# Gate products of a first block's merge, 20 of 32 made early in plain fp32 between the mixers' products and kept in DRAM

## The reference, cut to what matters

```python
h = x @ w_in                        # a_q .. d: inputs of four mixers; gate: 4 * 1024 columns
y = [mixer_a(...), mixer_b(...),    # each (512, 256): dilated attention, attention over 128 selected keys,
     mixer_c(...), mixer_d(...)]    # gated linear attention in chunks of 64, delta rule in chunks of 128
m = sum(sigmoid(gate[n]) * (y[n] @ w_branch[n]) for n in range(4))
x = layer_norm(ALPHA * x + m @ w_out)
```

## Time and profile before

| | |
|---|---|
| median of 3 runs | 3668.62 us (3665.24 to 3679.7) |
| profiled execution, its own time | 3665.9 us |
| its span | 3664.1 us, 33431 instructions |
| mean granted clock of TensorE | 0.882 |
| busy: TensorE, weight load | 3048.2 us (83%), 2257.0 us (62%) |
| busy: VectorE, ScalarE, GpSimd | 1734.7 us (47%), 646.1 us (18%), 1522.0 us (42%) |

### The profile page before, as it was taken

How to read it: one execution, slowest core, us unless ns; L and a number is a source line. 1 busy time by engine, 2 the same in 40 slices (tenths; PEclk the granted TensorE clock), 3 DMA queues, 4 the chain that set the end, 5 groups by cost and what they waited for, 6 DMA issues and landing times. The chain is left out here.

```text
span 3664.1 us, 33431 instructions
## 1 busy us (share of the span) xinstructions
PE 3048.2 (83%) x12858; PEld 2257.0 (62%) x12858; DVE 1734.7 (47%) x2065; ACT 646.1 (18%) x1005; POOL 1522.0 (42%) x430
## 2 busy tenths in 40 slices
PE   6939448899879999394689989999785689989998
PEld 5715237588556666273258867878562368768877
DVE  2174455444266666413464427860214554438840
ACT  0012210100135554303130010000102220010000
POOL 5600000277311111262017756767451037657776
PEclk9955569799979999696699999999896799989999
DMA  3300000122248887221202222222221212212223
GB/s 136 134 14 31 1 0 1 47 92 92 94 183 324 329 317 270 88 91 51 28 12 92 95 78 80 92 92 92 78 80 39 28 42 97 92 58 92 97 87 115
DMA packets 77126, 353.82 MB, mean 97 GB/s; under 512 B 30908, under 2 KB 31292, under 8 KB 38374
## 3 DMA queue, kind: packets, MB, share of 16 engines
q1 hardware_dynamic: 62824, 333.03, 25.4%
q10 hardware_dynamic: 2902, 10.13, 0.9%
q0 software_dynamic: 11232, 8.43, 0.8%
HBM read 357.39 MB, written 30.83 MB: 106 GB/s over the span
## 5 line engine op out<-in xcount | busy, mean ns | idle before, releaser
L129 POOL TENSOR_TENSOR w_hi<-w_raw,w_zero 128x2048 fp32r<-128x2048 f32 x174 | 627.6, 3607 | 1697.9 <-PE bank L156 1645.3
L156 PE MATMUL bank<-xh,w_hi 128*128 128x512 f32 x1864 | 750.1, 402 | 93.5 <-DVE xl L404 50.1
L132 POOL TENSOR_TENSOR w_lo<-w_raw,w_hi 128x2048 fp32r<-128x2048 f32 x174 | 813.2, 4674 | 13.7
L157 PE MATMUL bank<-xl,w_hi 128*128 128x512 f32 x1864 | 745.8, 400 | 0.0
L158 PE MATMUL bank<-xh,w_lo 128*128 128x512 f32 x1864 | 745.2, 400 | 0.0
L156 PEld LDWEIGHTS bank<-xh,w_hi 128*128 128x128 f32 x1864 | 355.3, 191 | 199.4 <-issue 44.0
L158 PEld LDWEIGHTS bank<-xh,w_lo 128*128 128x128 f32 x1864 | 355.3, 191 | 87.6
L157 PEld LDWEIGHTS bank<-xl,w_hi 128*128 128x128 f32 x1864 | 356.1, 191 | 84.8
L499 DVE TENSOR_TENSOR part<-sig,bank 128x512 f32<-128x512 f32 x96 | 66.1, 688 | 381.7 <-PE bank L158 381.3
L2121 DVE TENSOR_TENSOR fl<-work,fh 128x512 fp32r<-128x512 f32 x44 | 211.2, 4800 | 1.5
L536 DVE SCALAR_TENSOR_TENSOR res<-res,bank 128x512 f32<-128x512 f32 x40 | 27.5, 688 | 377.1 <-PE bank L158 377.1
(11 more groups left out here) (497 smaller groups left out, 4800.4 us busy)
## 6 DMA issues: line engine op xcount, KB each, us to landing
w_raw<-weights SPq DMA_DIRECT2D x216, 1024.0 KB, 4.8
raw<-weights SPq DMA_DIRECT2D x51, 1024.0 KB, 6.3
res<-weights SPq DMA_DIRECT2D x26, 1024.0 KB, 6.1
distance_bias<-distance_bias_once ACTq DMA_DIRECT2D x8, 512.0 KB
na_bias<-grid_bias SPq DMA_DIRECT2D x16, 240.0 KB, 7.0
strips<-distance_bias SPq DMA_DIRECT2D x8, 448.0 KB, 3.2
raw<-picked_rows SPq DMA_DIRECT2D x6, 512.0 KB, 5.9
tabs<-tables SPq DMA_DIRECT2D x2, 1408.0 KB, 6.4
```

The source lines that it names most:

```text
L129: pool.tensor_tensor(self.hi[:, s, :], self.raw[:, s, :], self.zero[:, 0:1].to_broadcast([128, CHUNK]), ALU.add).then_inc(self.rounded, 1)
L132: pool.tensor_tensor(self.lo[:, s, :], self.raw[:, s, :], self.hi[:, s, :].bitcast(F32), ALU.subtract).then_inc(self.split, 1)
L156: self.released(pe.matmul(out, hi, moving[0], start=start, stop=False))
L157: pe.matmul(out, hi, moving[1], start=False, stop=False)
```

## The change

`EARLY` holds 20 of the 32 gates, all u but those with u % 8 in (1, 4, 7). Their 160 blocks are now made by a new class, `EarlyGates`, as plain fp32 products of the unsplit weights in `w_raw` with an unsplit x, which SP loads (2 MB) as the selection begins. They are spread over the mixers' stages. TensorE gets 48 blocks behind the index products; in the attention 2, 1, 1, 2, 1, 1, 0 and 0 at the end of eight iterations in turn (32 in all); 16 behind mixer C's first product; 8 in C's head norm; and 16, 16 and 24 in mixer D's first three stages. ScalarE copies each finished gate out of bank 6 or 7 (bank 7 alone in the attention) at the end of its own part of the stage (in the attention after every eighth iteration), SP stores it to DRAM (256 KB) and after each second one loads the next chunk. A bank's next gate waits for the copy of the one before; in mixer D's third stage the three gates use banks 7, 6 and 7. That stage ends with SP's wait for the stores.

In the first merge ScalarE loads the kept gates from DRAM, four slots ahead, and applies the sigmoid in place; TensorE makes only the branch product of an early gate. `w_hi` and `w_lo` (32 KB of each partition) exist now only around project, the merge and what follows; in the mixers their room holds x and two copied gates. So project splits no chunk for the merge; the merge's first two chunks are loaded during `delta_chunks` and split when the merge begins. A barrier and the clearing of the new semaphores stand behind mixer D. The chunks in DRAM are laid out anew: 13 for project (the last one half padding), 10 early, 14 for the late gates, branches and `w_out`, 37 as before.

The diff, cut:

```diff
+LATE_GATES = (1, 4, 7)
+EARLY = [u for u in range(4 * KT) if u % 8 not in LATE_GATES]
+EARLY_CHUNKS = len(EARLY) // 2
...
+class EarlyGates:
...
+    def load(self, sp, chunk):
+        sp.dma_start(self.k.ws.raw[:, chunk % 2, :], self.k.ws.dram[self.first + chunk, :, :]).then_inc(
+            self.loaded[chunk % 2], 16)
+
+    def begin(self, sp):
+        sp.dma_start(self.x[:, :, :], self.k.dram["xT"]).then_inc(self.x_in, 16)
+        for chunk in range(2):
+            self.load(sp, chunk)
+
+    def fill(self, pe, n):
+        if self.blocks == 0:
+            pe.wait_ge(self.x_in, 16)
+        for b in range(self.blocks, self.blocks + n):
+            j, t = divmod(b, KT)
+            c = b // 16
+            if b % 16 == 0:
+                pe.wait_ge(self.loaded[c % 2], 16 * (c // 2 + 1))
+            if t == 0 and self.banks[j] in self.banks[:j]:
+                before = max(i for i in range(j) if self.banks[i] == self.banks[j])
+                pe.wait_ge(self.copied, before + 1)
+            mm = pe.matmul(self.k.bank[self.banks[j]][:, :], self.k.ws.raw[:, c % 2, 128 * (b % 16):128 * (b % 16) + 128],
+                           self.x[:, t, :], start=t == 0, stop=t == KT - 1)
+            if t == KT - 1:
+                mm.then_inc(self.made, 1)
+        self.blocks += n
+
+    def copy(self, act, n):
+        for j in range(self.n_copied, self.n_copied + n):
+            act.wait_ge(self.made, j + 1)
+            if j >= 2:
+                act.wait_ge(self.stored[j % 2], 16 * (j // 2))
+            act.activation(self.rows[:, j % 2, :], self.k.bank[self.banks[j]][:, :], ACT.Copy).then_inc(self.copied, 1)
+        self.n_copied += n
+
+    def move(self, sp, n):
+        for j in range(self.n_stored, self.n_stored + n):
+            sp.wait_ge(self.copied, j + 1)
+            sp.dma_start(self.out[j, :, :], self.rows[:, j % 2, :]).then_inc(self.stored[j % 2], 16)
+            if j % 2 and j // 2 + 2 < self.tiles // 2:
+                self.load(sp, j // 2 + 2)
+        self.n_stored += n
+
+    def end(self, sp):
+        assert self.n_stored == self.tiles
+        for s in self.stored:
+            sp.wait_ge(s, 8 * self.tiles)
+
+    def clear(self, nc):
+        assert self.n_copied == self.tiles and self.blocks == KT * self.tiles
+        for s in (self.x_in, self.made, self.copied, *self.loaded, *self.stored):
+            nc.sync.sem_clear(s)
+        nc.all_engine_barrier()
 
...
-                            last = ws.product(pe, g[:, :], (k.xh[:, t, :], k.xl[:, t, :]), t == 0, t == KT - 1)
-                        last.then_inc(gate_ready, 1)
+                        if u not in early:
+                            for t in range(KT):
+                                last = ws.product(pe, g[:, :], (k.xh[:, t, :], k.xl[:, t, :]), t == 0, t == KT - 1)
+                            last.then_inc(gate_ready, 1)
                         if u == 0:
...
             def _(act):
+                def ahead_load(e):
+                    act.dma_start(ahead[:, e % 4, :], early_dram[e, :, :]).then_inc(ahead_in[e % 4], 16)
+
+                for e in range(min(4, len(early))):
+                    ahead_load(e)
...
-                    act.wait_ge(gate_ready, u + 1)
+                    if u in early:
+                        e = early_before(u)
+                        act.wait_ge(ahead_in[e % 4], 16 * (e // 4 + 1))
+                        act.activation(ahead[:, e % 4, :], ahead[:, e % 4, :], ACT.Sigmoid).then_inc(sigmoid_ready, 1)
+                        if e >= 1 and e + 3 < len(early):
+                            act.wait_ge(banks_free, early[e - 1] + 1)
+                            ahead_load(e + 3)
+                        continue
+                    act.wait_ge(gate_ready, late_before(u) + 1)
                     if u >= 2:
                         act.wait_ge(banks_free, u - 1)
                     act.activation(sig[:, u % 2, :], k.bank[2 * (u % 2)][:, :], ACT.Sigmoid).then_inc(
...
+                        gate = ahead[:, early_before(u) % 4, :] if u in early else sig[:, u % 2, :]
...
+                if gates and s % 2 and s > 1:
+                    gates.move(sp, 1)
+            if gates:
+                gates.move(sp, 1)
...
+                if gates and i < n_units:
+                    gates.fill(pe, (2, 1, 1, 2, 1, 1, 0, 0)[i % 8])
...
+                if gates and i % 8 == 7:
+                    gates.copy(act, 1)
...
+            k.gates.fill(pe, 48)
...
+            k.gates.begin(sp)
+            k.gates.move(sp, 6)
...
+            k.gates.copy(act, 6)
...
+                k.gates.fill(pe, 24)
...
+            def _(sp):
+                k.gates.move(sp, 3)
+                k.gates.end(sp)
 
...
+        @block.sync
+        def _(sp):
+            k.ws.to_load = k.ws.n_loaded + SLOTS
+            k.ws.load(sp)
...
+        gate_dram = nc.dram_tensor("early_gates", (len(EARLY), 128, SEQ), F32, kind="Internal").ap()
+        gate_sems = ctx.enter_context(ExitStack())
+        k.gates = EarlyGates(k, nc, gate_sems, PROJECT_CHUNKS, len(EARLY),
+                             [7 if 6 <= j < 10 else 6 + j % 2 for j in range(len(EARLY))], gate_dram)
+        k.ws.limit = PROJECT_CHUNKS
         with memory(k, yb=(KT, SEQ)) as k.yb:
...
+                k.ws.blocks, k.ws.skipped = 16 * PROJECT_CHUNKS, EARLY_CHUNKS
+                k.ws.limit = FIRST_CHUNKS - EARLY_CHUNKS
+                with memory(k, whole_x=(KT, SEQ), gate_rows=(2, SEQ)) as (k.gates.x, k.gates.rows):
+                    mixers_ab(k, pj, av, bias_dram)
+                    mixer_c(k, pj, cv)
+                    mixer_d(k, pj, av, cv)
+                    k.gates.clear(nc)
+                    gate_sems.close()
+            with halves_of_weights(k):
+                merge(k, ALPHA, k.dram["xT"], EARLY, gate_dram)
+        ctx.enter_context(halves_of_weights(k))
```

More of the change, by code:

```diff
@@ L167, in product_tm, with halves_of_weights, __init__ @@
         return last
+@contextmanager
+def halves_of_weights(k):
+    with memory(k, w_hi=("r", SLOTS, CHUNK), w_lo=("r", SLOTS, CHUNK)) as (k.ws.hi, k.ws.lo):
+        yield
+class EarlyGates:
+    def __init__(self, k, nc, ctx, first_chunk, tiles, banks, out):
+        self.k, self.first, self.tiles, self.banks, self.out = k, first_chunk, tiles, banks, out
+        self.loaded = [ctx.enter_context(nc.semaphore(f"gate_w_loaded{s}")) for s in range(2)]
+        self.x_in = ctx.enter_context(nc.semaphore("gate_x_in"))
+        self.made = ctx.enter_context(nc.semaphore("gate_made"))
+        self.copied = ctx.enter_context(nc.semaphore("gate_copied"))
+        self.stored = [ctx.enter_context(nc.semaphore(f"gate_stored{s}")) for s in range(2)]
+        self.blocks = self.n_copied = self.n_stored = 0
+    def load(self, sp, chunk):
[44 more added lines that the diff above has]
+        nc.all_engine_barrier()
@@ L437, in _, with merge @@
                 run["vector"](dve, *sems)
-def merge(k, scale_residual, x_dram=None):
+def merge(k, scale_residual, x_dram=None, early=(), early_dram=None):
     ws = k.ws
+    n_late = 4 * KT - len(early)
     with memory(k, yh=("r", KT, SEQ), yl=("r", KT, SEQ), mh=("r", KT, SEQ), ml=("r", KT, SEQ), sig=(2, SEQ),
-                part=(2, SEQ)) as (yh, yl, mh, ml, sig, part):
-        ws.plan(KT * 40)
+                part=(2, SEQ), ahead=(4, SEQ)) as (yh, yl, mh, ml, sig, part, ahead):
+        ws.plan(KT * n_late + 8 * KT)
         with stage(k, "gate_ready", "sigmoid_ready", "branch_ready", "banks_free", "branch_rounded", "merge_order",
-                   "branch_split", "x_in") as (block, gate_ready, sigmoid_ready, branch_ready, banks_free, rounded,
-                                               order, branch_split, x_in):
+                   "branch_split", "x_in", "ahead_in0", "ahead_in1", "ahead_in2", "ahead_in3") as (
+                block, gate_ready, sigmoid_ready, branch_ready, banks_free, rounded, order, branch_split, x_in,
+                *ahead_in):
+            late_before = lambda u: sum(1 for v in range(u) if v not in early)
+            early_before = lambda u: sum(1 for v in range(u) if v in early)
             @block.sync
@@ L896, in _ @@
                           stop=True).then_inc(gate_ready, 1)
+                k.gates.fill(pe, 16)
+            @block.sync
+            def _(sp):
+                k.gates.move(sp, 2)
             @block.scalar
@@ L909, in _ @@
                 act.activation(ku[:, :], tmp[:, :], ACT.Exp).then_inc(decays_ready, 1)
+                k.gates.copy(act, 2)
             @block.vector
@@ L1002, in mixer_c @@
     head_norm(k, [dict(src=k.yb[:, 4 + p, :], scale=1.0 / 64, eps=k.eps[:, 1:2], finish=finish(p))
-                  for p in range(2)])
+                  for p in range(2)], k.gates)
 def mixer_d(k, pj, av, cv):
@@ L1027, in mixer_d, with _ @@
         with stage(k, "vector_order") as (block, order):
+            @block.tensor
+            def _(pe):
+                k.gates.fill(pe, 16)
+            @block.scalar
```

(10 more changed lines are left out.)

48 lines of the change are left out of this document (26 added, 22 removed).

## The result

The changed kernel takes 3554.37 us (median of 4 runs, 3552.13 to 3556.49) against 3668.11 in the runs beside it: a ratio of 0.968, 95% interval 0.966 to 0.971.

A forecast was written before the change was run, and what follows sets the result against it. TensorE was taken to bound the merge and, at a low clock, the attention; VectorE and ScalarE the small stages. -112.0 + 8 + 16.2 + 0 - 18 + 28.7 = -77.1 us gave 3592, range 3562 to 3642.

The forecast's parts named there:

- The price of a rounded block, 0.70: Merge: a block is three rounded products of 0.23 us each, so 160 blocks leaving save 112.0 us.
- the term for everything behind the first block: From `moe`'s start on: 0 us, as the change was said to touch only two parts of the first block.
- Merge, -87.8: First block's merge: -112.0 us for 160 blocks leaving, +8 for waits on VectorE, +16.2 for its start.
- Selection, 0: Selection: 48 early blocks end at 260 us, hidden behind VectorE's search until 266.2, so no change.
- Attention, -18: First block's attention: early blocks lift TensorE's clock to the high level, a head takes 10.75 us instead of 13.53.
- Small stages, +28.7: Mixers C and D: early blocks lengthen five small stages, less 2 us for a warm start, plus 1 for the barrier.
- The token shift: Mixer D: 16 early blocks take 13.9 us plus a copy of 0.6, making the stage 2.7 us longer.
- The last stage: Mixer D's third stage: 16 of 24 blocks hidden, the third tile waits for ScalarE's copy: +13.7 us, 9 to 18.
- Project, left out as "up to 2 us": Project: no longer splits a chunk for the merge, may end up to 2 us earlier; not counted in the sum.
- The attention did not stay low: Rival, attention: the clock stays at 0.50, +55 us instead of -18, 3665 in all; chance 0.11.
- early blocks ran at 0.87 us each where dense and warm: Rival, all early blocks: they run at the low clock everywhere, 1.73 us each, +79 us, 3747 in all; chance 0.05.
- VectorE was not the merge's bound: Rival, merge: VectorE's adds and casts wait out GpSimd's divide, 47 us of waits instead of 8, 3631; chance 0.09.

The follow-up runs named there:

- a_halves_on: The changed kernel with 32-byte pads around the split weights, putting them back on multiples of 64 bytes as before the change: 3594.93 us, ratio 0.980.
- b_halves_off: The kernel before the change with w_zero allocated ahead of w_hi, so the split weights lie 32 bytes off multiples of 64: 3619.72 us, ratio 0.986.
- a_banks8: The changed kernel with four pairs of banks instead of two in all merges: 3547.20 us, ratio 0.966.

## Why the prediction was wrong, step by step

**The price of a rounded block, 0.70, was the step that failed, and with it the term for everything behind the first block, which stood at nothing without a reason.** I took 0.70 from the earlier trace rows for what leaves the merge, and, unsaid, as the same for all that stays. It is 0.68 in the changed kernel. For the 160 blocks that leave, this changes nothing. Behind `moe`'s start some 6400 of these matmuls stand in dense rows; from start to start they take 1495.0 us before and 1451.9 in the changed kernel, 43 us or 6.7 ns each, where that part as a whole gained 38.2. "The change touches only two parts of the first block" was true of instructions and not of addresses. The diff showed that `w_hi` and `w_lo` were allocated elsewhere, and the part by part account never asked what that does to those who read them. Put back, the kernel takes 3594.93 us, 3 us from the forecast of 3592 and inside its range. That closeness is in part luck, as the terms below show.

**The sum within the first block** was -77.1, measured -72.3, and -78.2 in a_halves_on, which is the like comparison. There the attention gave 5.1 us too little (-12.9), and the merge 2.4, project 2.6 and the rest 1.2 more than forecast, so that the misses nearly cancelled. The terms:

*Merge, -87.8.* -84.8; -90.2 in a_halves_on, whose TensorE waits are 7.1 us in 3, against the 8 that I had stepped through. With closer matmuls VectorE is late more often: 13.0 us in 5. The faster clockwork of one engine went into waits for another. The start is as forecast, 725.17 - 708.94 = 16.2 us:

```profile
708.99 3.83 POOL L133 TENSOR_TENSOR w_hi<-w_raw,w_zero 128x2048 fp32r<-128x2048 f32 x1 [545.55 <-POOLq L245]
709.40 3.97 DVE L589 TENSOR_TENSOR yl<-yb,yh 128x512 fp32r<-128x512 f32 x1
...
712.90 4.82 POOL L136 TENSOR_TENSOR w_lo<-w_raw,w_hi 128x2048 fp32r<-128x2048 f32 x1
713.29 4.71 DVE L588 CAST yh<-yb 128x512 fp32r<-128x512 f32 x1
...
718.04 0.69 DVE L589 TENSOR_TENSOR yl<-yb,yh 128x512 fp32r<-128x512 f32 x1
...
725.17 0.79 PE L160 MATMUL bank<-yh,w_hi 128*128 128x512 f32 x1 [26.16 <-DVE yl L589]
```

Eight casts and eight differences cost 16 us because two of them end with GpSimd's two halves of the divide, 3.97 and 4.71 us instead of 0.69 and 0.43. The Trainium skill (SBUF — State Buffer, Terms, shared port pair) says that VectorE and GpSimd share a pair of ports by an exclusive lock and that the loser blocks for the whole instruction; these rows agree, for a cast too.

*Selection, 0.* Right: 84.48 us before and after.

*Attention, -18.* The likeliest case was the right one, the clock at 1.00, but the stage gave 9.6. In order of time, eight iterations (two heads) of TensorE:

```profile
286.10 1.98 PE L214 MATMUL bank<-whole_x,w_raw 128*128 128x512 f32 x4
288.01 0.70 PE L681 MATMUL bank<-pj 64*128 64x256 f32 x2
...
290.02 1.13 PE L214 MATMUL bank<-whole_x,w_raw 128*128 128x512 f32 x2
291.08 0.91 PE L681 MATMUL bank<-pj 64*128 64x384 f32 x2
...
308.82 0.55 PE L689 MATMUL bank<-consts,att_p 128*128 128x128 f32 x3 [0.89 <-DVE att_p L751]
...
309.98 1.98 PE L214 MATMUL bank<-whole_x,w_raw 128*128 128x512 f32 x4
```

From 286.10 to 309.98 are 23.9 us, 11.9 a head, where I had 10.75. The early blocks do not stand in a dense row: two take 1.91 us to the next instruction's start and a single one 1.06, 8.06 us for eight instead of 6.96. TensorE waits 0.89 us for VectorE where I allowed none. The rest is 7.5 a head, against my 7.3. Together 2.4 us per two heads, 9.5 in the stage. And the clock was at 1.00 for four of seven stretches only. The size differs between executions: 101.2 to 110.3 us in eight profiled ones that have the same code for this stage, the shortest at a clock of 0.96 over 262 to 366 us and the longest at 0.87. All are above the forecast's 96.

*Small stages, +28.7.* +31.5, and +28.2 in a_halves_on. The token shift was to start warm; it starts after 2.05 us of idle TensorE at the change of stage, and its 16 blocks take 15.67 us instead of 13.9:

```profile
433.24 15.67 PE L214 MATMUL bank<-whole_x,w_raw 128*128 128x512 f32 x32 [2.05 <-PEq L258]
...
448.95 0.60 ACT L225 ACTIVATE gate_rows<-bank 128x512 f32<-128x512 f32 x1 [6.27 <-PE bank L214]
```

(In a_halves_on, after an idle stretch just as long, they took 13.97 us: the clock was 1.00 from 432 to 436 us there, and 0.66 from 433 to 437 here.) The chunks' stage after the first of mixer C gained nothing from a warm start (forecast -2, here +1.9, and 0.0 in a_halves_on). The last stage came as told, step by step: 12.34 us of idle behind ScalarE, eight blocks, at first cold, in 9.10 us (I had 6 + 3.9 = 9.9), copy, store.

```profile
479.13 13.90 PE L214 MATMUL bank<-whole_x,w_raw 128*128 128x512 f32 x32
...
504.72 1.08 ACT L225 ACTIVATE gate_rows<-bank 128x512 f32<-128x512 f32 x2 [3.66 <-DVE pj L1284]
...
505.37 9.10 PE L214 MATMUL bank<-whole_x,w_raw 128*128 128x512 f32 x16 [12.34 <-ACT gate_rows L225]
...
514.50 0.60 ACT L225 ACTIVATE gate_rows<-bank 128x512 f32<-128x512 f32 x1 [8.70 <-PE bank L214]
...
518.37 1.06 PE L861 MATMUL bank<-consts,pj 128*128 128x128 f32 x8 [3.90 <-PEq L258]
```

It cost 10.2, not 13.7: VectorE's own chain was 2.2 us shorter, most of it because this stage's first products, 3.75 us in the earlier trace rows, now find a warm engine and take 1.95.

*Project, left out as "up to 2 us".* 5.0: 2.6 in a_halves_on, where no chunk is split for the merge; b_halves_off, which has the placement alone, gains 3.2.

**The rivals.** The attention did not stay low, early blocks ran at 0.87 us each where dense and warm (16 in 13.90 us), and VectorE was not the merge's bound; a_banks8 shows that directly.

**Not settled:** why both operands on a multiple of 64 is slower than both off; what exactly in the attention keeps or loses the clock, and why the later attention of the earlier trace rows rose to the high level without any dense product, where the first stayed low (its scores there are all 512 wide, those of the first attention 128 to 512).

## What to carry to other kernels

When a change moves an allocation, list every instruction that reads the moved tensors, also where no line changes, and compare the matmuls' start-to-start spacing in a stretch that the diff does not touch: if it differs, the comparison holds two changes. A run with the placement restored separates them for the price of a pad. And a gain at the start of a stage is worth only what the next wait leaves of it: look at both together before the edit is dropped, and at every call of the stage. The same edit gave nothing in the first merge and 6.7 us in each of the layers' merges.

## What the runs showed of the hardware

- The spacing of rounded 128 x 128 by 128 x 512 matmuls depended on the operands' byte offsets in SBUF: 0.2333 us with one of stationary and moving operand on a multiple of 64 bytes and the other 32 off, 0.2267 with both off, 0.229 with both on. Over this kernel the slow placement costs 41 to 47 us, some 1.1 to 1.3%, against both off.
- An attention in which TensorE is 97% busy with small products stayed at the 1.2 GHz level (0.50 for 86 us); with a plain 128 x 128 by 128 x 512 product in most iterations it ran mostly at 2.4 (0.87 to 0.96 over the stage), and with the same products in bursts of eight it did not (0.70). A later attention, also without any such product but with all its first scores 512 wide, rose to 1.00; what sets the two apart was not tested.
- Each of the divide's two instructions on GpSimd held one VectorE operation nearly to its own end (3.97 us instead of 0.69, 4.71 instead of 0.43). So the moment at which TensorE frees a weight slot sets when VectorE stalls: starting TensorE earlier delayed VectorE's last split by 7.6 us.
